# Squares added up on VectorE, and weight blocks loaded a phase ahead, in a two-layer hybrid trunk kernel

## The reference, cut to what matters

```python
def rms_norm(x, g):
    xf = x.astype(jnp.float32)
    y = xf * lax.rsqrt(jnp.mean(xf * xf, axis=-1, keepdims=True) + EPS)
    return (y * g.astype(jnp.float32)).astype(x.dtype)
...
    for l in range(DEPTH):
        ada = (cond @ ada_w[l] + ada_b[l])[:, None, :]
        sh1, sc1, g1, sh2, sc2, g2 = jnp.split(ada, 6, axis=-1)
        h = modulate(rms_norm(x, norm1_g[l]), sh1, sc1)
        x = x + g1 * mixer_sublayer(h, ...)
        h = modulate(rms_norm(x, norm2_g[l]), sh2, sc2)
        if l % 2 == 0:
            f = swiglu(h, ffn_w1[l // 2], ffn_w3[l // 2], ffn_w2[l // 2])
        else:
            f = moe_swiglu(h, ...)
        x = x + g2 * f
```

## Time and profile before

| | |
|---|---|
| median of 3 runs | 5590.35 us (5587.02 to 5594.34) |
| the profiled execution, its own time | 5590.09 us |
| its span in the trace | 5588.0 us |
| TensorE busy | 5298.8 us |
| VectorE busy | 2731.7 us |
| ScalarE busy | 1809.6 us |
| GpSimd busy | 757.4 us |
| mean granted clock of TensorE | 0.976 of full speed |

### The profile page before, as it was taken

How to read it: one execution, slowest core, us unless ns; L and a number is a source line. 1 busy time by engine, 2 the same in 40 slices (tenths; PEclk the granted TensorE clock), 3 DMA queues, 4 the chain that set the end, 5 groups by cost and what they waited for, 6 DMA issues and landing times. The chain is left out here.

```text
span 5588.0 us, 71451 instructions
## 1 busy us (share of the span) xinstructions
PE 5298.8 (95%) x29668; PEld 4435.1 (79%) x29669; DVE 2731.7 (49%) x2494; ACT 1809.6 (32%) x1615; POOL 757.4 (14%) x329
## 2 busy tenths in 40 slices
PE   7998999999999899899995999999999999999995
PEld 5676667778788667676774989999899998898985
DVE  7344257333524632623323545445575457854566
ACT  3113121132222220412112333334463336643354
POOL 1411111134444232021111000000000000000001
PEclk9999999999999899999997999999999999999997
DMA  5211124333635512021124555555595558965578
GB/s 178 79 46 51 38 77 114 110 94 109 189 95 144 181 59 67 20 61 46 43 94 161 190 194 194 190 188 195 201 333 189 187 197 304 354 220 183 193 248 301
DMA packets 810515, 854.53 MB, mean 153 GB/s; under 512 B 19250, under 2 KB 732082, under 8 KB 809906
## 3 DMA queue, kind: packets, MB, share of 16 engines
q1 hardware_dynamic: 802274, 820.18, 45.2%
q0 software_dynamic: 4608, 16.78, 0.8%
q10 hardware_dynamic: 3408, 14.68, 0.8%
HBM read 793.90 MB, written 57.67 MB: 152 GB/s over the span
## 5 line engine op out<-in xcount | busy, mean ns | idle before, releaser
L259 PE MATMUL banks<-h_hi,w_hi 128*128 128x512 f32 x2432 | 993.6, 409 | 76.2 <-DVE h_lo L738 34.1
L259 PE MATMUL banks<-e_x_hi,e_w_hi 128*128 128x256 f32 x3584 | 1016.2, 284 | 14.5 <-DVE e_w_lo L2233 12.2
L260 PE MATMUL banks<-e_x_lo,e_w_hi 128*128 128x256 f32 x3584 | 1015.3, 283 | 0.0
L261 PE MATMUL banks<-e_x_hi,e_w_lo 128*128 128x256 f32 x3584 | 1015.1, 283 | 0.0
L260 PE MATMUL banks<-h_lo,w_hi 128*128 128x512 f32 x2432 | 957.0, 394 | 0.0
L261 PE MATMUL banks<-h_hi,w_lo 128*128 128x512 f32 x2432 | 956.8, 393 | 0.0
L2233 DVE TENSOR_TENSOR e_w_lo<-e_raw,e_w_hi 128x2048 fp32r<-128x2048 f32 x340 | 764.1, 2285 | 192.4 <-ACT e_w_hi L2171 190.7
L2171 ACT ACTIVATE e_w_hi<-e_raw 128x2048 fp32r<-128x2048 f32 x340 | 647.3, 1911 | 503.9 <-PE banks L261 491.4
L259 PEld LDWEIGHTS banks<-e_x_hi,e_w_hi 128*128 128x128 f32 x3584 | 689.1, 192 | 17.3 <-DVE e_w_lo L2233 14.0
L260 PEld LDWEIGHTS banks<-e_x_lo,e_w_hi 128*128 128x128 f32 x3584 | 689.1, 192 | 0.1
L261 PEld LDWEIGHTS banks<-e_x_hi,e_w_lo 128*128 128x128 f32 x3584 | 689.1, 192 | 0.0
(11 more groups left out here) (307 smaller groups left out, 7043.3 us busy)
## 6 DMA issues: line engine op xcount, KB each, us to landing
e_raw<-in_moe_w_dram SPq DMA_DIRECT2D x510, 1024.0 KB, 5.9
w_raw<-in_ffn_w_dram SPq DMA_DIRECT2D x120, 512.0 KB, 3.9
w_raw<-in_w_in_dram SPq DMA_DIRECT2D x108, 512.0 KB, 4.1
f_ada_raw<-in_ada_w_dram SPq DMA_DIRECT2D x48, 512.0 KB, 5.0
g_ada_raw<-in_ada_w_dram SPq DMA_DIRECT2D x32, 512.0 KB, 4.1
e_io<-row_scratch SPq DMA_DIRECT2D x13, 1024.0 KB, 7.3
x_scratch<-x_res SPq DMA_DIRECT2D x24, 512.0 KB, 2.9
row_scratch<-stage SPq DMA_DIRECT2D x24, 512.0 KB, 2.6
```

The lines of the kernel that those rows point to most:

```text
L259: pe.matmul(out, wh, rh, start=first, stop=False)
L260: pe.matmul(out, wh, rl, start=False, stop=False)
L261: return pe.matmul(out, wl, rh, start=False, stop=last)
```

## The change

1. **Sums (back and dense).** ScalarE writes the square of tile 0 straight into an accumulator (`x_acc`, `acc`) and the others into `x_sq` or `sq`. VectorE adds each to the accumulator (`pile`), one tile behind its residual. TensorE sums the finished accumulator once for each half: at the end of back, in dense once after the first `up` of the second half and once at the end.
2. **Loads a phase ahead.** Blocks 0 and 1 of back are loaded at the start of attention, those of dense near the end of back, those of layer 1's front near the end of dense. In the later phase SyncE only raises `raw0` and `raw1` by 16. `inv` moves away from `w_raw[0]`.
3. **Layer 0's front.** GpSimd waits until the four adaLN blocks are added up, and only then makes its first subtractions.

```diff
@@ front_phase @@
             else:
-                load(0)
+                for b in range(2):
+                    sp.sem_inc((s.raw0, s.raw1)[b], 16)
                 for k in range(KT):
...
                     sp.dma_start(m.x[:, k, :], a.xs[P * k:P * k + P, :]).then_inc(x_in[k % 4], 16)
-            if not first:
-                load(1)
...
+            if first:
+                pool.wait_ge(s.added, NB)
             for j in range(3):
                 rest_w(j)
@@ attention_phase @@
-    inv = [m.place(f"attn_inv{l}{b}", [P, P], F32, m.W0 + 512 * b) for b in range(2)]
+    inv = [m.place(f"attn_inv{l}{b}", [P, P], F32, m.R + 196 * 1024 + 512 * b) for b in range(2)]
...
+            for b in range(2):
+                sp.dma_start(m.w_raw[b][:, :, :], w_view(a.w_in[l], C_GATE + P * b)).then_inc(s.w_in, 16)
             for t in range(2):
                 z_load(m.su[:, t, :], t)
...
+            sp.wait_ge(s.w_in, 16 * 2)
@@ back_phase @@
             for j in range(NBACK):
-                if j >= 2:
+                if j < 2:
+                    sp.sem_inc((s.raw0, s.raw1)[j], 16)
+                else:
                     sp.wait_ge(s.lo_ready, j - 1)
-                sp.dma_start(m.w_raw[j % 2][:, :, :], col(j)).then_inc((s.raw0, s.raw1)[j % 2], 16)
+                    sp.dma_start(m.w_raw[j % 2][:, :, :], col(j)).then_inc((s.raw0, s.raw1)[j % 2], 16)
...
+            if l % 2 == 0:
+                for b, w in enumerate((a.ffn_w1[l // 2], a.ffn_w3[l // 2])):
+                    sp.wait_ge(s.lo_ready, NBACK - 1 + b)
+                    sp.dma_start(m.w_raw[b][:, :, :], w_view(w, 0)).then_inc(s.next_in, 16)
+                sp.wait_ge(s.next_in, 32)
             for k in range(KT - 3, KT):
                 store(k)
...
-                    if j > NGATE:
-                        x_sum(j - NGATE - 1, half)
+            pe.wait_ge(s.r_root, 2)
             for half in range(NHALF):
-                x_sum(KT - 1, half)
+                pe.wait_ge(s.x_piled, 2 * (KT - 2) + half + 1)
+                pe.matmul(m.ps[:, 6 + half, :], cst[:, K_ONE:K_ONE + P], x_acc[half][:, :], start=True, stop=True).then_inc(s.x_summed, 1)
...
                 act.wait_ge(s.added, 2 * k + half + 1)
-                if k:
-                    act.wait_ge(s.x_summed, 2 * k + half - 1)
-                act.activation(x_sq[half][:, :], m.x[:, k, toks[half]], ACT.Square).then_inc(s.x_squared, 1)
+                if k >= 2:
+                    act.wait_ge(s.x_piled, 2 * (k - 2) + half + 1)
+                act.activation((x_sq if k else x_acc)[half][:, :], m.x[:, k, toks[half]], ACT.Square).then_inc(s.x_squared, 1)
...
+            def pile(k, half):
+                dve.wait_ge(s.x_squared, 2 * k + half + 1)
+                if k >= 2:
+                    dve.wait_ge(s.x_piled, 2 * (k - 2) + half + 1)
+                dve.tensor_tensor(x_acc[half][:, :], x_acc[half][:, :], x_sq[half][:, :], ALU.add).then_inc(s.x_piled, 1)
...
                                              in1=m.x[:, k, toks[half]], op0=ALU.mult, op1=ALU.add).then_inc(s.added, 1)
+                    if k >= 2:
+                        pile(k - 1, half)
+            for half in range(NHALF):
+                pile(KT - 1, half)
@@ dense_phase @@
+                    if half == 0 and f == 0:
+                        sp.sem_inc((s.raw0, s.raw1)[b], 16)
+                        continue
                     w_load(sp, s, m, LAP * half + 2 * f + b, b, w_view(w, P * f))
...
+            for b in range(2):
+                sp.wait_ge(s.lo_ready, NHALF * LAP + 1 + b)
+                sp.dma_start(m.w_raw[b][:, :, :], w_view(a.w_in[l + 1], FRONT[b])).then_inc(s.next_in, 16)
             store(NHALF - 1, KT - 1)
+            sp.wait_ge(s.next_in, 32)
...
                     up(half, f)
+                    if half and f == 0:
+                        total(0)
                 for j in range(KT):
                     down(half, j)
-                    if j:
-                        total(half, j - 1)
-                total(half, KT - 1)
+                if half:
+                    total(half)
...
+                    if j >= 2:
+                        pile(half, j - 1)
                     residual(half, j)
+                pile(half, KT - 1)
```

More of the change, by code:

```diff
@@ L898, in attention_phase @@
     with phase(nc, "v_up", "v_in", "scored", "maxed", "neg", "exped", "turned", "t_in", "valued", "inved", "o_in",
-               "z_in") as (block, s):
+               "z_in", "w_in") as (block, s):
         @block.sync
@@ L1067, in back_phase @@
     turns = [rq[:, 0, :], rq[:, 1, :], rk[:, 0, :], rk[:, 1, :]]
-    x_sq = [m.place(f"x_sq{l}{b}", [P, HALF], F32, at) for b, at in enumerate((R + 138 * KB, R + 194 * KB))]
+    x_acc = [m.place(f"x_acc{l}{b}", [P, HALF], F32, at) for b, at in enumerate((R + 138 * KB, R + 194 * KB))]
+    x_sq = [m.place(f"x_sq{l}{b}", [P, HALF], F32, R + at * KB) for b, at in enumerate((136, 140))]
     G1 = S_ADA + 48 * l + 16
@@ L1284, in beside @@
                     ada_total(g - 2 * ADA_BLOCK0 - 1)
-            def x_sum(k, half):
-                pe.wait_ge(s.x_squared, 2 * k + half + 1)
-                if k == 0:
-                    pe.wait_ge(s.r_root, 2)
-                pe.matmul(m.ps[:, 6 + half, :], cst[:, K_ONE:K_ONE + P], x_sq[half][:, :], start=(k == 0), stop=(k == KT - 1)
-                          ).then_inc(s.x_summed, 1)
             for j in range(NGATE):
@@ L1579, in dense_phase @@
     rstd = [m.rstd2[:, half, :] for half in range(NHALF)]
-    sq = [m.place(f"f_sq{l}{b}", [P, HALF], F32, m.R + (176 + 6 * b) * KB) for b in range(2)]
+    sq, acc = (m.place(f"f_{n}{l}", [P, HALF], F32, m.R + at * KB) for n, at in (("sq", 176), ("acc", 182)))
     tmp = [m.place(f"d_tmp{l}{b}", [P, HALF], F32, m.R + (168 + 2 * b) * KB) for b in range(3)]
@@ L1717, in _, with total @@
         def _(pe):
-            def total(half, j):
-                n = KT * half + j
-                pe.wait_ge(s.squared, n + 1)
-                pe.matmul(m.ps[:, 6 * (1 - half), :], cst[:, K_ONE:K_ONE + P], sq[n % 2][:, :], start=(j == 0), stop=(j == KT - 1)
-                          ).then_inc(s.summed, 1)
+            def total(half):
+                pe.wait_ge(s.piled, (KT - 1) * (half + 1))
+                pe.matmul(m.ps[:, 6 * (1 - half), :], cst[:, K_ONE:K_ONE + P], acc[:, :], start=True, stop=True).then_inc(s.summed, 1)
             def up(half, f):
@@ L1785, in hidden @@
                 dve.wait_ge(s.silu, n + 1)
+                if half and f == 1:
+                    dve.wait_ge(s.summed, 1)
                 dve.wait_ge(s.mm_done, LAP * half + 2 * f + 4)
```

24 lines of the change are left out of this document (16 added, 8 removed).

## The result

| | us |
|---|---|
| after, median of 4 runs | 5515.1 (5508.64 to 5521.51) |
| before, median of 4 runs | 5588.69 (5586.77 to 5594.34) |
| ratio | 0.9867, 95% interval 0.9855 to 0.988 |
| profiled execution of after: own time, span, mean granted clock | 5508.64, 5506.5, 0.980 |

A forecast was written before the change was run, and what follows sets the result against it. TensorE, busy 5298.8 of 5588.0 us, was taken as the bound, except at some phase starts waiting for weights. Terms of 22.5 + 9.4 - 0.7 + 10.2 + 2.5 + 13.0 + 1.9 = 58.8 us gave 5531.5, range 5522 to 5542.

The forecast's parts named there:

- Sum: Whole kernel: the terms of the edited places add up to 58.8 us gained, giving 5531.5 us.
- Sums in back: Back, both layers: TensorE loses most sums of squares, residuals come 5.44 us apart throughout; net gain 22.5 us.
- Sums in dense: Dense: fewer sums on TensorE between blocks gain 9.4 us; the longer tail at the end loses 0.7 us.
- Nothing is lost: Dense, block behind the 6-tile one: GpSimd's subtraction keeps 0.5 us of slack once the sum is gone.
- Attention into back: Start of back, both layers: weights already loaded, so ScalarE rounds at once; gains 4.85 and 5.33, together 10.2 us.
- the clock stays up: Rival, at the shorter gaps: TensorE's clock doesn't drop, 3 to 5 us more gained, 5524 us; chance 0.07.
- Back into dense: Start of dense: GpSimd's subtractions run earlier but still meet the first scalings; gain 2.5 us, bounds 0 and 4.7.
- Dense into front: Start of layer 1's front: earlier weights shorten TensorE's largest single gap, 22.75 us; gain 13.0 us.
- VectorE waiting for x: Layer 1's front, sign of being wrong: scalings wait for x; 3 us lost if loads lag 0.4 us a tile.
- Layer 0's front: Layer 0's front: GpSimd's later subtractions free the adaLN additions but meet the first scalings; gain 1.9 us, bounds 0 and 4.1.
- GpSimd as the bound: Rival, mainly dense: GpSimd's subtractions bound TensorE once the sums are gone, 5549 us; chance 0.07.
- VectorE's piles waiting: Rival, back: VectorE's additions wait for squares behind roundings, stalling residuals and TensorE; 5616 us at 3 us each; chance 0.02.

The follow-up runs named there:

- the group with after again: Kernels measured on one chip with before, among them the unedited changed kernel once more: 5511.87 us, ratio 0.9866.
- the four kernels with stands: Before (5588.7 us), before with all of the change but the sums (5561.0), and the changed kernel with 50 (5537.3) or 178 (5540.2) semaphore increments on VectorE.
- the 16 increments: Kernel before, with 16 increments of an unused semaphore put into VectorE's program in dense: 5571.05 us, ratio 0.9966.
- the version with shorter tails: Changed kernel with half 1's weight rounding moved ahead in dense, and TensorE adding the last tile's square itself in three tails: 5502.14 us, ratio 0.9845.
- all kernels of the table: Before, after, before with parts of the change, and either with unused semaphore increments on VectorE or TensorE; medians from 5513.0 to 5588.7 us.
- after with 50, 135, 150 and 178 increments: Changed kernel with that many unused semaphore increments in VectorE's program in dense: 5537.34, 5513.78, 5513.02 and 5540.15 us.

## Why the prediction was wrong, point by point

- **The step that failed is "Sum".** It adds up the edited places and so sets the experts' part to 0, with no term and no rival for it. It was worth 21.9 us in the profiled executions: 18.0 by VectorE's place (2472.7 - 2454.6) and 3.8 by TensorE's (2454.6 - 2450.8). With it the sum would be 58.8 + 21.9 = 80.7 us; the two profiled spans differ by 81.5. That this fits so well is partly luck, since the profiled execution of after is the fastest of its four and 3.7 us of its lead ahead of the experts are the clock's. By the medians (73.6 us, and 75.1 in the group with after again) the edited places gave some 52 to 53 us, by the traces without the clock's part 57, where the forecast has 58.8.
- **That the place turned out well is luck too.** The edit was made for other reasons. With 50 instructions more, VectorE's loop would have lain as before, and the time would have been 5537.34 us, inside the predicted range.
- **How 80 us of stands became 18 of time.** VectorE has slack in the loop, and most stands fall where TensorE has enough prepared. It costs most around the four short items (the rows of 128x256 above): 2.4 to 4.0 us each of before against after, 12.9 together. Six of the eight full items lose 0.7 to 1.5 us, 6.7 together, TensorE's own waits among them, and the end of the loop 2.3. TensorE's waits on `e_w_lo` in the loop, behind the first matmul, are 17 with 23.1 us in before and 10 with 13.6 us in after. In the four kernels with stands the granted clock also fell to half for 3.4 us two to four times in the loop, some 12 us behind such waits, about 1.5 us each (a 128x256 matmul every 0.213 us there and 0.120 at full speed); in none of the others did it. With the 16 increments TensorE's gaps in the loop fall from 34.7 to 24.5 us, and the gap behind the loop, ahead of combine, from 15.8 to 13.6. 10.2 + 2.3 + 3.0 us of the 18.0 are found so; the other 2.5 I did not split.
- **Sums in back: right.** 5.44 us throughout. Both back phases with their starts gave 31.2 us, 32.9 without the clock's part; the forecast is 32.7.
- **Sums in dense: right in size, two steps off.** The tile is 15.70 us as foretold (16.56 before), and the tail lost 0.75 us (forecast 0.7). "Nothing is lost" at the seam of the halves was wrong: the idle time there grew from 2.34 to 4.92 us, since the rounding waits behind the square there, whether or not TensorE has a sum to do. In the other direction goes the clock, 5.8 us: TensorE worked 20.5 us at half clock in before's dense phase and 8.2 in after's. Among these are two stretches of 3.4 us behind the adaLN sums of before (263.2 and 645.5 us into dense), which are not in after. So dense gave 15.0 us, not 11.2, and 9.2 without the clock's part. The first of the two stretches stands in all three kernels that have their sums on TensorE and in one of the ten others, the second in three and in four. So the sums may have to do with them, but they come and go between executions of after itself, and the 5.8 us are not the edit's to claim.
- **Attention into back: right.** TensorE starts 3.6 us after the phase's start in both layers, 8.5 and 9.0 before: 4.9 and 5.4 us (forecast 4.85 and 5.33). The clock was still partly down, 0.65 in the first 4 us of TensorE (0.52 in the earlier trace rows), so of the rival "the clock stays up" little came. The window of after (us; busy PE, PEld, DVE, ACT, POOL; granted clock; DMA share; GB/s):

```profile
475.77:479.77 4.00, 4.00 (x12) 3.20 (x13) 0.00 (x0) 3.97 (x4) 0.00 (x0) 0.65 0.54 132
```

- **Back into dense: right in number, in part by luck.** The first marks of the down stage stand 2.55 us earlier (forecast 2.5), but TensorE's waits up to there are only 1.45 us shorter. The rest is the clock's, at half for 17.1 us at the start of before's dense phase and 10.2 of after's, and the term has no clock. Subtractions and scalings collide as said: the two scalings took 3.50 us.
- **Dense into front: right.** 13.1 us at TensorE's first matmul (forecast 13.0). The part as a whole gave 11.7. The loss is in the first block: TensorE waits there for `h_lo` at 1885.92 and 1888.08, 0.24 and 1.19 us in after, 0.36 in all in before; the clock takes another 0.4. The second comes behind the scaling of 1886.61, which waited 0.74 us for x. The prediction had named VectorE waiting for x as a sign of being wrong; it is there, at a cost of about 1 us, not the 3 us of its text.
- **Layer 0's front: right.** The adaLN sums take 4.69 us all four times and the first scalings 3.45 us beside the subtractions; TensorE starts at 58.68, forecast 58.9. So the exclusion of the two engines is moved, as argued.
- **GpSimd as the bound, VectorE's piles waiting:** the first hardly showed, the second not at all. Of TensorE's three waits on `w_lo` in dense, 5.4 us, the seam is 4.9. The two others, 0.23 and 0.24 us inside the down stages, are new: that sign of being wrong showed, at 0.5 us in all. None of TensorE's waits is released by a residual of back inside its tiles.
- **The range.** It was made from the bounds of the terms alone, and a whole missing term isn't in them. Could it have been seen? Yes, in the trace of before: the idle times of VectorE ahead of `e_act`, whose named releaser had long been done; 63 of q14's packets in the experts' part, though the loop runs the same code in every pass; and the 5 us behind a branch that jumps nowhere but to its own loop. I had listed what the change does to VectorE's program and didn't ask what the length of that program does.

## What to carry to other kernels

An edit that changes how many instructions stand ahead of a loop with a runtime branch moves the loop among its code blocks. Before you cost such an edit, look at the instruction queues of part 3 and at the time between the loop's branch and the next instruction; if a pass loads code anew, a few empty instructions ahead of the loop are worth more than most tuning (here 16 of them gave 18 us), and any later edit can lose it again. When a change comes out better than its terms, cut both traces by phase and look first at the phases that it doesn't touch. Then take the clock's part out of each phase before you call a term right: here it hid a loss of 2.6 us at the seam of dense, and it made the version with shorter tails look faster than it is.

## What the runs showed of the hardware

- **Code is loaded in blocks, and a loop may be one block too long.** VectorE's come as packets of 8192 bytes: an edit of its program alone took q14 from 98 packets to 42. A loop of 296 instructions had one stand of 3.8 us or none at places 13 to 97 of 128, and 19 stands of some 91 us in all at place 125, with about 56 packets more. TensorE's loop of 1734 instructions in blocks of 16384 bytes had 21 packets more at place 205 of 256 than at 35. By the count, VectorE's loop lies over three blocks at places 13, 75 and 82 and over four at 125, TensorE's over seven at 35 and eight at 205. At place 97 it would be four, yet nothing stood. If the loop lies some 9 to 13 instructions lower on the chip than by the compiled count, all kernels of the table fit; that offset was inferred and not measured by itself.
- The Trainium skill, "Runtime: NRT & Kernel Launch", section "Instruction fetch mechanics", says that a taken branch whose target isn't among the blocks held makes the engine wait for a load, and that code comes in blocks of 16 KiB of which most engines hold two. The runs agree with the first: a packet of instructions starts within the stand, and the stand lasts 4.9 to 5.3 us in 11 of 14 passes. On the second they differ: VectorE's blocks are of 8 KiB, and a loop over three of them has no stands.
- A stand lasts 4.9 to 5.3 us behind the branch back (11 of 14 passes), and in seven passes 4.6 to 4.7 us more behind a later branch of the pass (L2387 in before).
- At half clock a 128x512 matmul follows the other every 0.427 us (2115 to 2121 us of before), at full clock every 0.227 (2105 to 2112). With 47% of TensorE's time at half taken out, the part ahead of the experts is 2957.0 to 2959.4 us in seven executions that raw lie at 2990.3 to 3002.9.
- The time of one kernel varies through the clock. The six profiled executions whose code up to the experts does the same work (after twice, and after with 50, 135, 150 and 178 increments) reached the first expert matmul at 2990.3 to 2998.8 us, with 146 to 169 us at half clock ahead of it, while the experts' part of the four without stands is 2450.8 to 2451.0. A part that is cut out of the trace told 3.8 us apart, which the medians did not.
